# Gathered U rows for 64 tokens instead of 32 in the expert layers of a decoder trunk

## The reference, cut to what matters

```
q = (h @ w_q) per head (8 heads, two halves of 128)
s = q . keys                       # 128 scores per half
s_top, i_top = top_k(s, 16)        # each half
best, pos = top_k(16 x 16 sums, 16)
idx, gate = expert number (of 16384), softmax(best)
act = gelu(u_tab[idx] . h)         # 16 experts x 8 heads per token
y = sum(gate * act * v_tab[idx])
```

## Time and profile before

| what | number |
|---|---|
| runs | 3166.78 us median of 3 (3166.71 to 3169.4) |
| span of the profiled execution, first to last instruction | 3168.2 us |
| PE, DVE, ACT, POOL busy over the span | 97%, 83%, 42%, 67% |
| granted clock of PE, mean | 0.990 |
| DMA | 883.09 MB, 279 GB/s mean |
| one load of a U tile | 512 KB |
| one store of activations | 176 KB |
| one piece of the routing | 1024 KB |
| chain that ended last, PE's share; lines 2113, 2069, 2079 | 36%; 16%, 14%, 3% |

### The profile page before, as it was taken

The page is one execution under the profiler, slowest core; times in us unless marked ns, Lnnn a source line. Parts: engine busy times, 40 slices in busy tenths (PEclk is TensorE's granted clock), DMA queues, the critical chain, the costliest instruction groups (busy, mean ns, idle before and its releaser), DMA issues. The chain is left out here.

```text
span 3168.2 us, 57859 instructions
## 1 busy us (share of the span) xinstructions
PE 3080.1 (97%) x21401; PEld 2643.9 (83%) x21401; DVE 2642.7 (83%) x4447; ACT 1338.7 (42%) x2400; POOL 2111.8 (67%) x1366
## 2 busy tenths in 40 slices
PE   8999998999999999999999899999999999999998
PEld 3437887799999999888888677999999998888886
DVE  8875664689999995999999656799989958999997
ACT  0125453333346775333333423333367753333333
POOL 1213444478877777888888604788777778888884
PEclk9999999999999999999999999999999999999999
DMA  9950002588878999999999614788789999999995
GB/s 341 328 200 24 4 5 100 167 289 285 274 242 322 389 389 370 371 350 351 366 350 349 208 57 158 275 286 275 237 318 384 396 369 376 348 350 366 351 349 177
DMA packets 379378, 883.09 MB, mean 279 GB/s; under 512 B 39513, under 2 KB 208017, under 8 KB 370962
## 3 DMA queue, kind: packets, MB, share of 16 engines
q1 hardware_dynamic: 284690, 536.14, 47.8%
q0 software_dynamic: 94464, 343.97, 30.0%
HBM read 780.21 MB, written 98.62 MB: 277 GB/s over the span
## 5 line engine op out<-in xcount | busy, mean ns | idle before, releaser
L2069 PE MATMUL peer_acc<-peer_hhi,peer_uhi 128*128 128x352 f32 x2048 | 673.2, 329 | 1.1 <-POOL peer0same_ulo L2319 0.5
L2069 PE MATMUL peer_acc<-peer_hlo,peer_uhi 128*128 128x352 f32 x2048 | 662.4, 323 | 0.0
L2380 DVE SCALAR_TENSOR_TENSOR peer_row<-peer_row,peer_acc 128x1024 f32<-128x1024 f32 x320 | 385.6, 1206 | 19.7 <-DMA peer_row<-in_pe_u,peer_idx 14.0
L2319 POOL TENSOR_TENSOR peer1same_ulo<-ahead_u,peer_uhi 128x1024 fp32r<-128x1024 f32 x128 | 308.7, 2413 | 127.3 <-ACT peer_uhi L2162 124.0
L2319 POOL TENSOR_TENSOR peer0same_ulo<-ahead_u,peer_uhi 128x1024 fp32r<-128x1024 f32 x128 | 309.6, 2420 | 125.8 <-ACT peer_uhi L2162 121.6
L2069 PEld LDWEIGHTS peer_acc<-peer_hhi,peer_uhi 128*128 128x128 f32 x2048 | 387.9, 189 | 2.7 <-POOL peer0same_ulo L2319 0.8
L2069 PEld LDWEIGHTS peer_acc<-peer_hlo,peer_uhi 128*128 128x128 f32 x2048 | 386.7, 189 | 1.0 <-issue 0.5
L2348 POOL TENSOR_TENSOR peer1lsame_vlo<-peer1l_v,peer1l_vhi 128x1024 fp32r<-128x1024 f32 x128 | 308.6, 2411 | 68.1 <-ACT peer1l_vhi L2211 67.6
L2348 POOL TENSOR_TENSOR peer0lsame_vlo<-peer0l_v,peer0l_vhi 128x1024 fp32r<-128x1024 f32 x128 | 308.4, 2410 | 67.9 <-ACT peer0l_vhi L2211 67.4
L2391 DVE SCALAR_TENSOR_TENSOR peer_acc<-peer_row,peer_p_g,peer_acc 128x1024 f32<-128x1024 f32 x254 | 325.1, 1280 | 20.1 <-DMA peer_row<-in_pe_v,peer_idx 19.6
L2069 PE MATMUL peer_acc<-peer_hhi,peer0same_ulo 128*128 128x352 f32 x1024 | 331.7, 324 | 0.0
(11 more groups left out here) (516 smaller groups left out, 7094.1 us busy)
## 6 DMA issues: line engine op xcount, KB each, us to landing
ahead_u<-in_pe_uT SPq DMA_DIRECT2D x256, 512.0 KB
peer0l_v<-in_pe_v SPq DMA_DIRECT2D x128, 512.0 KB
peer1l_v<-in_pe_v SPq DMA_DIRECT2D x128, 512.0 KB
activations<-peer_gel SPq DMA_DIRECT2D x256, 176.0 KB
rw_g<-in_ada POOLq DMA_DIRECT2D x60, 512.0 KB
routing<-peer0m_wb SPq DMA_DIRECT2D x24, 1024.0 KB
peer0l_wt<-routing SPq DMA_DIRECT2D x64, 384.0 KB
routing<-peer1m_wb SPq DMA_DIRECT2D x24, 1024.0 KB
```

Of the source, the lines that this page charges most:

```text
L2069: mm = pe.matmul(ub[e % 2][:, 0:UD], a, h[:, k, 0:UD], start=(n == 0), stop=(n == 3 * KT - 1))
L2319: g.tensor_tensor(ulo[:, q].rearrange("p k e -> p (k e)"), u[:, q].rearrange("p k e -> p (k e)"), uhi[:, e % NH].bitcast(F32).rearrange("p ...
L2380: v.scalar_tensor_tensor(out=row[:, m % NG], in0=row[:, m % NG], scalar=1.0, in1=h_own if mine else h_g, op0=ALU.mult, op1=ALU.mult, accum ...
```

## The change: what it does

`OWN` becomes 64 and `COPIES` 2, so a gather of own tokens serves two slots and there are 64 own dots a layer: 192 dots instead of 160. U products, gelu and the store of activations cover 320 tokens. The head stage has 12 dots for each head from head 2 on, the stage between has 16 own dots instead of 8 (eight before the first group and eight beside the first groups), which leaves 96 for the block stage (84 before). The ramp moves to PSUM at group 10 instead of 6. POOL may issue three gathers a tile, in one place four. ACT multiplies in all four gates of a group, and DVE's `tensor_scalar` of line 2484 goes.

```
-H_AT, U_AT, MIXER_H_AT = 82688, 40192, 78336
+H_AT, U_AT, MIXER_H_AT = 82432, 40448, 78336
-OWN = 32
-COPIES = 4
+OWN = 64
+COPIES = 2
-HEAD_DOTS = 10
-BETWEEN_DOTS = 8
+HEAD_DOTS = 12
+BETWEEN_DOTS = 16
-ACT_GATES = 3
+U_AT_ONCE, LAST_AT_ONCE = 3, 4
-EXP_AT, TURN_AT, OWN_BY = 4, 3, 6
+EXP_AT, TURN_AT, OWN_BY = 4, 3, 10
...
-                return AT_DOTS - BETWEEN_DOTS + max(0, min(e - AT_BETWEEN - HEAD_OWN, HEAD_OWN))
+                return AT_DOTS - BETWEEN_DOTS + max(0, min(2 * (e - AT_BETWEEN - 4), HEAD_OWN))
...
                 def spread_group(n):
-                    pe.wait_ge(gated, ACT_GATES * (n + 1))
-                    pe.wait_ge(i_made, n + 1)
+                    pe.wait_ge(gated, G * (n + 1))
...
-                    for q in range(ACT_GATES):
+                    for q in range(G):
                         a.activation(hot_i[:, n % 2, q], pair[n % 2][:, 0, q], ACT.Copy,
                                      scale=slotT[:, 0, n * G + q:n * G + q + 1]).then_inc(gated, 1)
...
-                    if n * G == UD:
-                        dve.wait_ge(own_taken, 1)
-                    for q in range(n * G + ACT_GATES, (n + 1) * G):
-                        ins = v.tensor_scalar(hot_i[:, n % 2, q % G], numbers, slotT[:, 1, q:q + 1], slotT[:, 0, q:q + 1], ALU.is_equal,
-                                              ALU.mult)
-                    ins.then_inc(i_made, 1)
```

More of the change, by code:

```diff
@@ L1786, in phase_peer @@
         DOTS = SLOTS + OWN_SLOTS
+        assert HEAD_DOTS == 3 * HEAD_OWN // 2
         MIXED = FIRST_DOTS + (HEADS - 2) * HEAD_DOTS + BETWEEN_DOTS
@@ L1815, in dot_of @@
             if q < HEADS - 2:
[L1816 to L1819, removed]
+                three, r = divmod(i, 3)
+                if r:
+                    return True, HEAD_OWN * q + 2 * three + r - 1
+                return False, FIRST_DOTS + q * (HEAD_DOTS - HEAD_OWN) + three
             if m < MIXED:
@@ L1912, in phase_peer @@
         whi_made, wlo_made, iota_made = sem("whi"), sem("wlo"), sem("iota")
-        j_made, i_made, spread_done, taken = sem("hot_j"), sem("hot_i"), sem("spread"), sem("taken")
+        j_made, spread_done, taken = sem("hots"), sem("spread"), sem("taken")
         w_stored = [sem("w0_stored"), sem("w1_stored")]
@@ L2336, in _ @@
                         low_query(n + 1, r // 2)
-                    for _ in range(HEAD_OWN if e == AT_BETWEEN + MOVE_LAST + 2 + NH else AT_ONCE):
+                    for _ in range(LAST_AT_ONCE if e == AT_BETWEEN + MOVE_LAST + 2 + NH else U_AT_ONCE):
                         if e >= FETCH_LAG and n_u < min(NG + dots_by(e - FETCH_LAG), ready_by(e)):
@@ L2477, in _ @@
                         dve.wait_ge(spread_done, n - 1)
-                        dve.wait_ge(gated, ACT_GATES * (n - 1))
+                        dve.wait_ge(gated, G * (n - 1))
                     v.tensor_tensor(pair[n % 2], numbers.unsqueeze(1).unsqueeze(1).to_broadcast([P, 2, G, P]),
                                     slotT[:, 1:3, n * G:(n + 1) * G].unsqueeze(3).to_broadcast([P, 2, G, P]), ALU.is_equal).then_inc(j_made, 1)
-                    if n * G == UD:
-                        dve.wait_ge(own_taken, 1)
-                    for q in range(n * G + ACT_GATES, (n + 1) * G):
-                        ins = v.tensor_scalar(hot_i[:, n % 2, q % G], numbers, slotT[:, 1, q:q + 1], slotT[:, 0, q:q + 1], ALU.is_equal,
-                                              ALU.mult)
-                    ins.then_inc(i_made, 1)
                     if n == A_TILE * (OWN_GELU_AT + 2):
```

## The result

The changed kernel takes 3250.01 us in the median (3244.61 to 3251.54, 4 runs), the kernel before, run beside it, 3166.77 (3166.71 to 3169.4, 4 runs): ratio 1.0257, 95% interval 1.0244 to 1.0269. The forecast was 3181, range 3142 to 3214: right in sign, and 36 us beyond the range. The profiled execution has a span of 3247.9 us, 79.7 more than before; the granted clock is 0.981 in the mean (0.990 before).

What follows compares the result with a forecast made beforehand. PE was taken to set the end, with DVE and DMA close behind. A +14, B 0 and C -7 gave +7 a layer, +14 in both, on the 3168.2 us span: 3182, so 3181 for the median; range 3142 to 3214.

Steps and rivals of the forecast that it cites:

- PE: U matmuls of 320 columns cost 146.8 ns, not 160.1; 0.32 us less a tile, 82 us in both layers.
- A: Layer start to `slots_made`, on DVE's path: +14 us a layer, bounds -3 to +33.
- c: Stretching of DVE's instructions by POOL's subtractions in a head: 5.2 us today, 6.2 forecast, giving heads of 43.0 us.
- the two dots at 2.4 us: Heads from 2 on: two more dots at 1.21 us each raise DVE's own work from 34.4 to 36.8 us.
- The first rival: Heads: stretching is only how DVE idles; with c = 2.8 a head stays 39.6 us, total 3143; chance 0.27.
- B: `slots_made` to group 10: DVE +3.1 us against its idle time, so 0 a layer (-2 to +5).
- C: Group 10 to the V stage, 303.8 us: -7 us a layer (-14 to +3).
- All fit, each barely: In C, per tile of 5.32 us: DVE 5.0, ACT 4.7, POOL 5.2; the DMA does not fit.
- The fourth rival: Block stage: gathers and so DVE's pairs come late, C is +3, total 3201; chance 0.12.
- The DMA term: In C: 19.1 MB per eight tiles against 17.8 at 418 GB/s; 5.4 MB added, 12.9 us of transfer.
- side estimate of 26 us a layer for C: HBM limit of about 358 GB/s a core would make C cost 26 us a layer; given no chance of its own.
- all pairs near 418: Sign for C: pairs of tiles all near 418 GB/s, none near 319, with tiles of about 5.5 us.

Runs made afterwards that it cites:

- narrow products alone: Kernel before with U products, gelu and stores 320 columns wide, no dots added, tokens 320 to 351 left out: 3161.16 us, ratio 0.9978.
- changed, two dots fewer: Changed kernel with the sixth and twelfth dot of each head from head 2 on replaced by a constant, gathers kept: 3245.69 us, ratio 1.0229.
- changed, subtraction halved: Changed kernel with POOL's subtraction over four of eight slabs in tiles 14 to 55, PE's work unchanged: 3201.66 us, ratio 1.0106.
- 336 columns: Kernel before with U products, gelu and stores 336 columns wide, half the narrowing: 3169.26 us, ratio 0.9992.
- 63% with twelve dots: Changed kernel with U products 352 columns wide again, the last 32 computed but unused: 3246.27 us, ratio 1.0240.
- four gates on ACT: Kernel before with all four gates of a group on ACT and DVE's line 2484 gone: 3168.66 us, ratio 1.0000.
- lag 1: Changed kernel with block-stage gathers issued by the dots of the tile before, not three tiles before: 3205.01 us, ratio 1.0119.
- the move: On the changed kernel with lag 1, own dots moved to their place at block tile 8 instead of 14: 3198.06 us, ratio 1.0089.
- half the rows: Changed kernel with lag 1 and the move, block-stage gathers fetching only the rows of partitions 0 to 63: 3184.26 us, ratio 1.0055.

## Why the prediction was wrong

**PE: right.** 147 ns a matmul and 3.52 us a tile, measured 146.7 and 3.52.

**A: the size near by luck, and a step of the sum wrong.** +14 forecast, +9.5 measured. Heads 2 to 6 added 11.6 us where the sum has 17, and head 7 lost 0.9 where it has 2.4 more. DVE is the pacer at 95.5% (262.75 of 275), and PE's idle time is released by POOL line 2319 (15.9 us in 8 waits from 2000 to 2270 us), as I said. A head is indeed DVE's own work plus c. Summed over the instructions of head 3, with c as the time beyond each one's shortest length in any of these runs, and with DVE never idle:

| kernel | head 3, us | own work | c |
|---|---|---|---|
| before | 39.6 | 34.3 | 5.3 |
| changed | 41.9 | 36.3 | 5.6 |
| narrow products alone | 41.6 | 34.3 | 7.3 |
| changed, two dots fewer | 41.5 | 34.4 | 7.1 |
| changed, subtraction halved | 37.3 | 36.3 | 1.0 |

What failed is the step that priced the two dots at 2.4 us and set c beside them as something apart. With the narrower tile c is 7 without the dots and 5.6 with them: the dots fill time in which DVE would be held anyway, and are worth 0.3 to 0.4 us a head. The narrowing, which I had down as a gain, makes the long head by itself, and the longer head of my forecast came out near the measured one because one error stood for the other. What drives c is POOL's subtraction: halve it, and c goes. POOL subtracts 2.41 us of every 3.52 (68%) where it had 2.41 of 3.84 (63%), but this share alone does not order the kernels: 65% at 336 columns has heads of 41.1, and 63% with twelve dots heads of 39.7 to 42.9. Which instruction comes to lie under a subtraction counts too. The first rival's idea, that the stretching is only how DVE idles, is refuted by the narrow kernels: PE could go at 37.4 and 38.5, and DVE did not follow.

**B: about +3.6** (5.0 in layer 0) for 0 (-2 to +5). Inside its bounds; no run took it apart.

**C: the step that failed.** I wrote "All fit, each barely", summed the busy time of four engines and the bytes, and got -7 (-14 to +3); it was +26. The sum has no latency in it. The fourth rival named the mechanism, late gathers, and I priced it at +3 and set it aside with "eight rows of lead are about 19 us". That is where it went wrong: the ring has eight rows, but `dots_by(e - 3)` holds POOL's list back by the dots of three tiles. That is 3 x 84/45 = 5.6 rows before and 3 x 96/43 = 6.7 after. POOL's list runs a tile or two ahead of DVE's, which gives some back; measured, 4.7 rows were under way or unused at an issue before, and 4.1 after. In time, from issue to dot, 12.17 us before and 9.58 after, where a row took about 9 to land (medians of 8.7 to 9.3 in the three kernels with these schedules whose traces show landings: narrow products alone, four gates on ACT, halved in the heads). Before there were some 3 us to spare, after next to none. The lead was in the trace of before, in POOL's and DVE's timelines, and I did not measure it; the landing is not in that trace. Issue by lag 1 takes the step out, and with the move C is -1.4 in layer 1 and +3.6 in layer 0, near my upper bound and not at -7. The DMA term fits: tiles stop at 5.74, where 19.1 MB at 418 GB/s give 5.71. That the DMA is then the limit is not shown, since half the rows moved a tile only to 5.61. The seven microseconds of room that I counted on top were not to be had.

One number of the prediction may mislead: its side estimate of 26 us a layer for C, by a DMA limit to which it gave no chance, meets the measured 26.4. That is chance. With lag 1 the same 116.7 MB (tiles 71 to 127) pass in 22 us less.

The half clock was in no term. The granted clock stood at 1.2 GHz for 37.5 us of layer 1's U stage after the change and for 3.4 before; 13.7 of the 37.5 lie in the heads and 17.1 from tile 72 on. At half the clock at most half of such a time is lost work, so at most 8.6 of C's 26.4 us. Part of it lies in waits that would be there anyway, and no run separated it.

**Signs.** Of those I named, the tile of 3.52 us, PE's idle time behind line 2319 and DVE above 93% came; 43 us between ends of line 2453 came as 42; "all pairs near 418" did not come, the stage swings between 217 and 422 GB/s from 2360 us on, and together with lag 1 that points away from the DMA's rate and to a loop.

Open: what sets the blocks once rows are in time and half as large (5.61 us a tile, where PE needs 5.31); why heads at 352 columns with twelve dots vary between 39.7 and 42.9; what makes part B longer; and the share of the clock below that bound.

## What to carry to other kernels

"Every engine fits" is no forecast for a stage with a ring: compare the lead of each prefetch, in us from issue to use as the schedule allows it and not as the buffer does, with its landing time, and do it again when more uses fall into a tile. Where an instruction of one engine holds those of another, a stage's length belongs to the pattern of the two and not to their work alone: a shorter step elsewhere can break it, so test the one edit that changes the rhythm alone before adding up the rest. Taking work from a pacing engine that is only just the slowest is worth what the next one allows, here 7 of 82 us.

## What the hardware showed beside that

- An operation on 128x32 numbers with both inputs in SBUF took 4.92 us behind two subtractions of POOL in a row; it did not get in between them. A `tensor_scalar` with one input did (2.35 us, the kernel before).
- The granted clock fell to 1.2 GHz inside an idle time of PE of 5.39 us, and in the heads of the changed kernel four times at idle times of 2.5 to 2.7 us.
- Two transfers of 16 KB took 17.72 and 22.55 us to land while the queues carried 399 GB/s (2414 to 2437 us of the kernel with lag 1); gathers of 512 KB beside them took 10 in the median.
- Gathers of 64 rows kept the DMA engines as busy (0.99 at 314 GB/s) as gathers of 128 (1.03 at 417 GB/s).
